# Dilated heads: sums of squares by a strip of ones in four column tiles, turned back by four transposes

## What is computed

```python
qh = _rms(q.reshape(b, S, ATTN_HEADS_2, ATTN_HEAD_DIM).astype(f32), q_norm_w)
kh = _rms(k.reshape(b, S, ATTN_HEADS_2, ATTN_HEAD_DIM).astype(f32), k_norm_w)
# _rms: xf * lax.rsqrt(jnp.mean(xf * xf, axis=-1, keepdims=True) + EPS) * w
```

## Time and profile before

| | us |
|---|---|
| median of 3 timed runs | 3342.87 (3342.13 to 3344.57) |
| span of the profiled execution | 3339.8 |
| outside the span, by the median | 3.1 |
| dilated stage in the profiled execution | about 1570 to 2120 |

### The profile page before, as it was taken

One profiled execution on the slowest core, in us unless ns is written; L12 is line 12 of the kernel. 1 busy time (PEld: TensorE's weight loads), 2 busy tenths in 40 slices (PEclk: granted clock), 3 DMA queues, 4 the chain that ended last, 5 costly groups with the idle time before them and its releaser, 6 DMA issues.

```text
span 3339.8 us, 39742 instructions
## 1 busy us (share of the span) xinstructions
PE 3236.2 (97%) x15586; PEld 2682.9 (80%) x15586; DVE 1466.1 (44%) x2210; ACT 864.1 (26%) x1410; POOL 1154.4 (35%) x880
## 2 busy tenths in 40 slices
PE   6999999998999899999999999999999999999999
PEld 4778888887787677888888888888788878888887
DVE  6775666566445875543211332325314651313131
ACT  3545444444222231300223223201101210101020
POOL 2342122211366321223222222344335763434352
PEclk9999999999999999999999999999999999999999
DMA  3221001000243220144222122421113221111112
GB/s 134 95 73 44 26 26 39 27 31 26 76 145 120 66 87 32 51 161 155 63 61 67 56 72 64 131 66 51 51 45 120 95 82 45 51 49 47 51 46 81
DMA packets 92210, 234.25 MB, mean 70 GB/s; under 512 B 7680, under 2 KB 33920, under 8 KB 91920
## 3 DMA queue, kind: packets, MB, share of 16 engines
q1 hardware_dynamic: 53504, 186.67, 17.2%
q10 hardware_dynamic: 38544, 45.24, 4.3%
HBM read 212.84 MB, written 19.04 MB: 69 GB/s over the span
## 4 chain that ended last, share of the span: by engine, by line
PE 90%; DVE 7%; ACT 2%; issue 1%; DMA 0%; ACTq 0%; DVEq 0%
PE proj_bank L226 23%; PE proj_bank L228 23%; PE proj_bank L227 23%; PE aux_banks L226 2%; PE aux_banks L227 2%; PE aux_banks L228 2%; PE aux_banks L799 2%; PE aux_banks L880 2%; PE aux_banks L806 1%; PE aux_banks L2223 1%; PE aux_banks L1791 1%; PE aux_banks L2251 1%; PE aux_banks L587 1%; DVE aux_banks L1672 1%; PE aux_banks L2272 1%
## 5 line engine op out<-in xcount | busy, mean ns | idle before, releaser
L226 PE MATMUL proj_bank<-h_hi,slab_hi 128*128 128x512 f32 x2816 | 1120.6, 398 | 18.5 <-DVE h_lo L414 8.6
L228 PE MATMUL proj_bank<-h_hi,slab_lo 128*128 128x512 f32 x2816 | 1102.6, 392 | 0.0
L227 PE MATMUL proj_bank<-h_lo,slab_hi 128*128 128x512 f32 x2816 | 1101.4, 391 | 0.0
L247 POOL CAST slab_hi<-slab_raw 128x1024 fp32r<-128x1024 f32 x292 | 311.4, 1066 | 2140.1 <-PE proj_bank L228 1634.4
L251 POOL TENSOR_TENSOR slab_lo<-slab_raw,slab_hi 128x512 fp32r<-128x512 f32 x584 | 843.2, 1465 | 23.4
L226 PEld LDWEIGHTS proj_bank<-h_hi,slab_hi 128*128 128x128 f32 x2816 | 532.1, 189 | 138.0 <-issue 11.1
L228 PEld LDWEIGHTS proj_bank<-h_hi,slab_lo 128*128 128x128 f32 x2816 | 531.5, 189 | 113.7
L227 PEld LDWEIGHTS proj_bank<-h_lo,slab_hi 128*128 128x128 f32 x2816 | 532.7, 189 | 107.9 <-issue 2.2
L226 PE MATMUL proj_bank<-ffn_hi,slab_hi 128*128 128x512 f32 x512 | 199.2, 389 | 0.4 <-issue 0.4
L227 PE MATMUL proj_bank<-ffn_lo,slab_hi 128*128 128x512 f32 x512 | 199.2, 389 | 0.0
L228 PE MATMUL proj_bank<-ffn_hi,slab_lo 128*128 128x512 f32 x512 | 199.2, 389 | 0.0
(11 more groups left out here) (380 smaller groups left out, 4183.1 us busy)
## 6 DMA issues: line engine op xcount, KB each, us to landing
slab_raw<-wts SPq DMA_DIRECT2D x292, 512.0 KB, 3.5
ada_w<-ada_w SPq DMA_DIRECT2D x40, 384.0 KB, 3.2
ada_w_early<-ada_w SPq DMA_DIRECT2D x24, 384.0 KB, 3.5
ssd_decay_rows<-decay_sums ACTq DMA_DIRECT2D x16, 512.0 KB, 3.9
dil_rows<-dilated_out ACTq DMA_DIRECT2D x12, 520.0 KB, 7.7
x_first<-xT SPq DMA_DIRECT2D x4, 1024.0 KB, 9.2
x<-xT ACTq DMA_DIRECT2D x4, 1024.0 KB, 6.6
x_kept<-x ACTq DMA_DIRECT2D x16, 256.0 KB, 2.7
```

Of the source, the lines that this page charges most:

```text
L226: pe.matmul(bank, k.whi[:, slot, wk, :], hi[:, xk, cols], start=first and a == 0, stop=False)
L227: pe.matmul(bank, k.whi[:, slot, wk, :], lo[:, xk, cols], start=False, stop=False)
L228: mm = pe.matmul(bank, k.wlo[:, slot, wk, :], hi[:, xk, cols], start=False, stop=last and a == len(ks) - 1)
L247: pool.tensor_copy(k.whi[:, to], k.raw[:, slot]).then_inc(k.s_hi, 1)
```

## The change

The sums of squares are made the other way round. The stationary operand becomes a strip of 32 columns of ones (`ones_strip`), the squares move, 512 columns at a time. The two halves of q and the two of k go to four strips of 32 partitions of one PSUM bank (`sums_of`), each strip holding 32 equal rows of 512 sums. VectorE scales and adds EPS over the whole 128x512 bank into SBUF (`sum_rows`). Four transposes turn the four 128-column blocks (`turned_sums`, another bank), and ScalarE's root reads one column of every 32 of them (`sum_cols`) into the same 16 columns as before.

In TensorE's order `square_sums` stands where statistics 0 stood, with all four matmuls, and `turn_sums` where statistics 1 stood, behind half 4. ScalarE's root waits for the transposes (`s_colsum`) and no longer for VectorE (`s_var`); the transposes wait for `s_var`. `sum_rows` lies at F + 29, where `mix` still stands at the stage's opening, so VectorE waits for `s_kept` ahead of its first statistics. A memset makes the strip of ones.

```diff
+STRIP = P // 4
+    ones_strip = k.at("dil_ones", F + 111.875, [P, STRIP])
+    sum_rows = k.at("dil_sum_rows", F + 29, [P, HALF])
+    sums_of = lambda i, c: k.aux[(2 * i + c) * STRIP:(2 * i + c + 1) * STRIP, 0, :]
+    turned_sums = k.aux[:, 1, :]
+    sum_cols = turned_sums.rearrange("p (b t w) -> p t b w", t=P // STRIP, w=STRIP)[:, :, :, 0]
+    s_colsum = k.sem("dil_sums_turned")
...
-        def statistics(j, g, i):
+        def square_sums(j, g):
 
             pe.wait_ge(s_evac, j * 18 + (6 * g + 4 + 2))
             pe.wait_ge(s_pt, j * 3 + (g + 1))
-            for b in range(TT):
-                mm = pe.matmul(k.aux[:, 0, i * TT + b:i * TT + b + 1], sq[:, i, b * P:(b + 1) * P], k.ones, start=True, stop=True)
-            if i == 1:
-                mm.then_inc(s_stat, 1)
+            for i in range(2):
+                for c in range(2):
+                    mm = pe.matmul(sums_of(i, c), ones_strip, sq[:, i, c * HALF:(c + 1) * HALF], start=True, stop=True)
+            mm.then_inc(s_stat, 1)
+
+        def turn_sums(j, g):
+
+            pe.wait_ge(s_var, j * 3 + (g + 1))
+            for b in range(HALF // P):
+                mm = pe.transpose(turned_sums[:, b * P:(b + 1) * P], sum_rows[:, b * P:(b + 1) * P], k.ident)
+            mm.then_inc(s_colsum, 1)
...
             if more:
-                statistics(*after(j, g), 0)
+                square_sums(*after(j, g))
                 half(*after(j, g), 4)
...
-                statistics(*after(j, g), 1)
+                turn_sums(*after(j, g))
                 half(*after(j, g), 5)
                 spread(*after(j, g))
...
-        statistics(0, 0, 0)
+        square_sums(0, 0)
         half(0, 0, 4)
-        statistics(0, 0, 1)
+        turn_sums(0, 0)
         half(0, 0, 5)
...
         def root(j, g):
-            act.wait_ge(s_var, j * 3 + (g + 1))
-            act.activation(stat, stat, ACT.Sqrt).then_inc(s_root, 1)
+            act.wait_ge(s_colsum, j * 3 + (g + 1))
+            act.activation(stat.rearrange("p (t b) -> p t b", t=P // STRIP), sum_cols, ACT.Sqrt).then_inc(s_root, 1)
...
-        dve.sem_inc(s_pt, 1)
+        dve.memset(ones_strip, 1.0).then_inc(s_pt, 1)
...
             dve.wait_ge(s_stat, j * 3 + (g + 1))
-            dve.tensor_scalar(stat, k.aux[:, 0, 0:2 * TT], 1.0 / P, EPS, ALU.mult, ALU.add).then_inc(s_var, 1)
+            dve.tensor_scalar(sum_rows, k.aux[:, 0, :], 1.0 / P, EPS, ALU.mult, ALU.add).then_inc(s_var, 1)
...
+        dve.wait_ge(s_kept, 16 * KT)
         statistics(0, 0)
         norm(0, 0)
```

## The result

| | median, us | runs | ratio to the kernel before |
|---|---|---|---|
| before | 3343.44 | 3342.13 to 3344.57 | |
| changed | 3316.77 | 3315.78 to 3318.53 | 0.9922 (95%: 0.9909 to 0.9935) |

A forecast was written before the change was run, and what follows sets the result against it. TensorE's instruction stream was taken to bound the dilated stage. Sums 27.6 us plus transposes 5.2 us minus removed groups 41.1 us gave -8.3 us, about 3335 us by the median; range 3318 to 3352 us.

The forecast's parts named there:

- What bounds the kernel: Dilated stage: TensorE's instruction stream is the clock, busy 538.2 of 545 us; what leaves it moves the end equally.
- What is removed: Dilated stage: 24 groups of one-column matmuls on TensorE at 1.71 us, 41.1 us, all on the path.
- five steps: Sums on strips: each strip's first pass starts with the previous strip's second pass; 2.30 us a head, chance 0.42.
- lower bound: Sums on strips: all four strips side by side, two passes deep, 1.02 us a head.
- rival B: Sums on strips: full overlap, 1.02 us a head, -23.7 us, 3319 us; chance 0.20 for full or nearly full overlap.
- X: Length of each head's block of strip sums on TensorE, forecast 2.30 us, with 2.14 and 2.46 as ends.
- break-even of 2.98 us: Length of a head's block of sums at which added TensorE work equals the 3.42 us removed.
- rival A: Sums on strips: eight passes in a row, 3.42 to 3.75 us a head, 3348 to 3352 us; chance 0.30.
- Going into and out of strips: Around each head's sums: emptying the array on entry and exit, each at most 0.16 us.
- The transposes: Ahead of half 5: four added transposes a head on TensorE, 0.44 us, 5.2 us over twelve heads.
- The clock: Opening head: the fall to 1.2 GHz may go (-1.6 us), stay or move; 0 in the sum.
- C: Transposes wait for VectorE or spread for root, giving back up to 0.7 us a head, 3343 us; chance 0.03.

The follow-up runs named there:

- one-strip run: Against the changed kernel, all four sum matmuls keep 32 columns of ones but go to the same strip; 3345.1 us in one run.
- in pairs: Changed kernel with eight sum matmuls of 256 columns instead of four of 512, ordered strip 0, strip 0, strip 1, strip 1, and so on; 3314.4 us.
- in rounds: Changed kernel with eight sum matmuls of 256 columns instead of four of 512, ordered strips 0, 1, 2, 3 and again; 3315.7 us.

## Why the prediction was wrong

**What bounds the kernel** held: no new wait, and every microsecond out of TensorE's stream came off the span.

**What is removed** held: 24 groups at 1.71 us, 41.1 us; with it the sum of the stretch, below, closes to 0.3 us. Giving back the strips but keeping all the rest gives back everything (3343.95 us).

**The block of sums was the failed step.** I wrote that the second pass of a matmul goes to the same strip, waits for the first, and that matmuls begin in program order, so the next strip starts one step late: five steps, 2.30 us. The first half is true (one-strip run, 0.43 us from pass to pass). The second isn't, across strips: all four start within 20 ns, and even whole matmuls queued on a strip don't hold the others (1.02 us in pairs). The order of starts in the trace of before couldn't carry that step: there every matmul has the full width, so nothing could have overtaken. By the measured 1.00 us the term is 12 x 1.00 = 12.0 us and not 12 x 2.30 = 27.6, so the gain is 15.6 us larger than I made it. My lower bound of 1.02 us was the value to within 0.02, and rival B the case that came, at a chance of 0.20. That the kernel got faster was forecast, but every X under the break-even of 2.98 us gives that; the sign says nothing for the five steps.

The strict first in, first out order that TensorE: Matmul & The Clock Gate of the Trainium skill, section Part 3: Packing small matmuls, states for matmuls is not what the pairs show between strips, if the stream reaches TensorE in program order. Its other rule there, that weight loads overlap only with another row group, would have given rival A, and the trace contradicts it: the four strips share all 128 rows and their eight loads are done in 0.16 us, most of them while the first passes stream. The prediction had the evidence against that rule in its own text, since full-width loads lie beside streaming in every projection. The page's 2.38x for three strips was the better guide; four strips took 1.00 us where one strip took 3.55, 3.6x.

**Going into and out of strips** was bounded with 0 to 0.33 us, and the one-strip run gives 0.31 us. I had put one half of it into X; it shows as 0.1 us ahead of the block and in its tail.

**The transposes** take 0.35 us and not 0.44: their starts are 0.11 us apart, three distances for four of them, and the projection starts 0.03 us behind the last. That is 1.1 us less over 12 heads, which the 0.1 us ahead of the strips uses up.

**The clock** went the way I had left out of the sum: -1.6 us.

Together, for the stretch: -8.3 forecast, -15.6 (X), -1.6 (clock) is -25.5 us; measured 156.7 - 181.9 = -25.2 us. The median moved by 26.7 us, with an interval of 21.7 to 30.4, and the span of the profiled execution by 24.7; what these differ from the stretch by lies outside it and has no cause here.

**Rivals A and C** fall: A would have been right with all sums in one strip; C needed the cover of VectorE or the root to be gone, and it is 4.8 and 3.3 us, as worked out (4.8 and 3.4).

**The range** ended at 3318 us, 1.2 us above the measured median. Rival B and the clock together, both of which came, give 3342.87 - 23.7 - 1.6 = 3317.6 us by the prediction's own terms, and their 25.3 us are what the stretch shows (25.2). So the end had the right mechanism in it and no room beyond it: kernels with the same stretch differ by 3 us in the runs above.

## What to carry to other kernels

A block of matmuls with 32 output rows on different strips of the array costs what the busiest strip streams, plus about 0.3 us for going in and out; in the two orders tried here, with equal loads, the order was worth 0.02 us. Count passes first: with fp32, two slow passes per matmul make strips worth 2.2 us a head against full width, while single-pass operands at full width reach the same 1.0 us with no strips, and strips with single-pass operands 0.33 us. What single-pass operands do to the precision of the sums isn't weighed here. And where a cost has no row in the trace, a sequence rule read from rows that could not have shown its violation bounds nothing: give the lower bound real weight, and leave room beyond it for what moves outside the stage.

## What the runs showed of the hardware

- Four fp32 matmuls of 512 columns on four strips: 1.00 us; on one strip 3.55 us; at full width 3.03 us to the next start, with about 0.4 us more in the matmul behind.
- The same block in bf16, one pass per matmul, on four strips: 0.33 us; four single fp32r passes at full width: 1.01 us.
- A second matmul queued on a busy strip shifts the next strip's start by about 6 ns: 13 ns apart in pairs, 6.6 ns in rounds, 3.3 ns in bf16.
- Entering and leaving the strips: 0.31 us together.
- Work of one column behind this 1.2 us wait is followed by 3.41 us at the 1.2 GHz level (2 of 2 traces); streaming work in its place keeps 2.4 GHz (8 of 8), although TensorE's busy time in the stretch with the wait is the same 2.23 us before and after.
